# State-space stage of a hybrid block: decays from running sums spread by DMA, y and z kept with features on partitions, one gate and norm per group

## What is computed

```python
u = rmsnorm(h, mix_pre_norm)
q, k, v, z, xbc, dt_raw, g_a, g_b = split(u @ w_in)
y_attn = banded_sink_attention(rope(q), rope(k), v, sinks) @ w_attn_out
# ssd_mixer
x, B, C = split(silu(causal_dwconv(xbc)))
dt = softplus(dt_raw + dt_bias);  a_cs = cumsum(dt * -exp(a_log))
y  = (C B^T * exp(a_cs[l] - a_cs[s]) masked) @ (x * dt)     # diagonal part
y += (C @ previous_state) * exp(a_cs)                       # part from the state
y += x * d_skip
y  = y * silu(z);  y = y * rsqrt(mean(y^2 over the group) + eps) * norm_w
# then
merged = sigmoid(g_a) * y_attn + sigmoid(g_b) * (y @ w_ssd_out)
h = h + rmsnorm(merged @ w_out)
h = h + rmsnorm(silu(conv(gate)) * conv(value) @ w_down)    # channel mixer
```

## Time and profile before

| | |
|---|---|
| median of 3 runs | 1079.98 us (1079.81 to 1080.94) |
| the profiled execution | 1081.87 us, of which the span of instructions is 1079.8 us |
| PE busy | 1059.3 us, 98% of the span |
| DVE, ACT, POOL busy | 645.3, 454.7, 124.6 us |
| groups G = 0 to 3 end (us of the span) | 126.8, 233.0, 339.1, 444.3 |
| granted TensorE clock | 1.00 of 2.4 GHz throughout |

### The profile page before, as it was taken

One profiled execution on the slowest core, in us unless ns is written; L12 is line 12 of the kernel. 1 busy time (PEld: TensorE's weight loads), 2 busy tenths in 40 slices (PEclk: granted clock), 3 DMA queues, 4 the chain that ended last, 5 costly groups with the idle time before them and its releaser, 6 DMA issues.

```text
span 1079.8 us, 13848 instructions
## 1 busy us (share of the span) xinstructions
PE 1059.3 (98%) x5353; PEld 888.5 (82%) x5353; DVE 645.3 (60%) x867; ACT 454.7 (42%) x714; POOL 124.6 (12%) x196
## 2 busy tenths in 40 slices
PE   8999999999999999999999999999999999999997
PEld 8888888878888887788888888788888888888886
DVE  4897777776777777842433233466666666651214
ACT  4664456445654565532321213363434344431112
POOL 6013300330033013200000003120000000000001
PEclk9999999999999999999999999999999999999999
DMA  6321132114202420232233243413424233323211
GB/s 189 118 69 30 40 117 69 30 40 123 81 13 58 138 79 1 79 100 95 78 117 99 96 162 129 137 41 78 116 78 115 80 110 84 110 92 110 82 74 78
DMA packets 108426, 95.39 MB, mean 88 GB/s; under 512 B 12175, under 2 KB 98523, under 8 KB 108379
## 3 DMA queue, kind: packets, MB, share of 16 engines
q1 hardware_dynamic: 108379, 94.74, 28.7%
HBM read 92.63 MB, written 2.10 MB: 88 GB/s over the span
## 4 chain that ended last, share of the span: by engine, by line
PE 85%; DVE 8%; ACT 3%; POOL 2%; issue 1%; DMA 1%; POOLq 0%; DVEq 0%; SPq 0%; ACTq 0%
PE ps L1200 18%; PE ps L1201 18%; PE ps L1202 18%; PE ps L1207 8%; PE ps L1208 8%; PE ps L1209 8%; PE ps L1486 2%; DVE wlo L793 1%; ACT whi L449 1%; DVE conv L902 1%; PE ps L1427 1%; PE ps L1239 1%; POOL xdtd L403 1%; PE ps L1498 1%; PE ps L1478 1%
## 5 line engine op out<-in xcount | busy, mean ns | idle before, releaser
L793 DVE TENSOR_TENSOR wlo<-raw,whi 128x2048 fp32r<-128x2048 f32 (+2 forms) x83 | 188.5, 2272 | 209.8 <-ACT whi L449 209.8
L1200 PE MATMUL ps<-uhi,whi 128*128 128x512 f32 x640 | 249.6, 390 | 0.1
L1202 PE MATMUL ps<-uhi,wlo 128*128 128x512 f32 x640 | 249.1, 389 | 0.0
L1201 PE MATMUL ps<-ulo,whi 128*128 128x512 f32 x640 | 249.0, 389 | 0.0
L449 ACT ACTIVATE whi<-raw 128x2048 fp32r<-128x2048 f32 (+2 forms) x83 | 155.2, 1871 | 175.5 <-PE ps L1209 93.0
L1200 PEld LDWEIGHTS ps<-uhi,whi 128*128 128x128 f32 x640 | 120.2, 188 | 25.1 <-DVE zg L1011 0.2
L1202 PEld LDWEIGHTS ps<-uhi,wlo 128*128 128x128 f32 x640 | 120.1, 188 | 24.9
L1201 PEld LDWEIGHTS ps<-ulo,whi 128*128 128x128 f32 x640 | 120.2, 188 | 24.6
L1207 PE MATMUL ps<-whi,uhi 128*128 128x512 f32 (+2 forms) x304 | 115.3, 379 | 2.0 <-DVE wlo L793 1.8
L1209 PE MATMUL ps<-wlo,uhi 128*128 128x512 f32 (+2 forms) x304 | 112.6, 370 | 0.0
L1208 PE MATMUL ps<-whi,ulo 128*128 128x512 f32 (+2 forms) x304 | 112.6, 370 | 0.0
(11 more groups left out here) (230 smaller groups left out, 1466.9 us busy)
## 6 DMA issues: line engine op xcount, KB each, us to landing
raw<-in_w_in_dram SPq DMA_DIRECT2D x24, 1024.0 KB
raw<-in_w_up_dram SPq DMA_DIRECT2D x44, 512.0 KB
raw<-in_w_down_dram SPq DMA_DIRECT2D x11, 1024.0 KB
raw<-in_w_in_dram SPq DMA_DIRECT2D x16, 512.0 KB
raw<-in_w_ssd_out_dram SPq DMA_DIRECT2D x8, 1024.0 KB
raw<-in_w_attn_out_dram SPq DMA_DIRECT2D x4, 1024.0 KB
raw<-in_w_out_dram SPq DMA_DIRECT2D x4, 1024.0 KB
yT<-in_x_dram SPq DMA_DIRECT2D x4, 512.0 KB, 4.9
```

The source lines that it names most:

```text
L793: dve.tensor_tensor(wlo[sl][:, 0:width] if into is None else into, raw[sl][:, 0:width], h.bitcast(F32), ALU.subtract).then_inc(s["lo_done" ...
L1200: pe.matmul(bank(b)[:, span], hi_[:, k, c], ah[:, span], start=first and k == 0, stop=False)
L1201: pe.matmul(bank(b)[:, span], hi_[:, k, c], al[:, span], start=False, stop=False)
L1202: ins = pe.matmul(bank(b)[:, span], lo_[:, k, c], ah[:, span], start=False, stop=last and k == KD - 1)
```

## The change

- **z** is made by `features` (four tiles of 128 features, all tokens), one in each of four places; two blocks of 8 x 256 in place of 4 x 512. Gate and tanh work on features.
- **Decays.** The running sums of one group, tile and head are written once to a scratch in DRAM (`sum_scr`, and their exponentials beside them), and DMAs copy a row of 8 x 128 of them to all 128 partitions (`sums_bc`, `grow_bc`, 512 KB each). ACT makes `decay_m` from it (`gains`: 8 Relu of 128 x 128 with the token's own sum as bias, then 2 Exp). L1404, L1405, `seg_hi` and `seg_lo` are gone.
- **The part from the state** uses C scaled by POOL per head (`c_dec`, 128 x 1024, 12 times), so that it can be accumulated with the diagonal part. Both are now 8 matmuls with weights 64 wide (`state` or `xdt`) and 128 columns streamed (`products`), and heads take turns between the lower and the upper 64 output partitions.
- **y** comes out with features on partitions, so `turn_y` is gone. One DVE instruction a tile adds the skip term (made by ACT, `skip_x`) and stores y.
- **Gate and norm** are made once per group, in the next group's first blocks: `gate_y` (4 DVE), `square_y` (4 ACT), `sum_squares` (3 DVE), `norm_sums` (4 matmuls of one column), mean, root on POOL, two DMAs through DRAM that spread the roots, `normalize` (4 DVE).
- **Softmax**: Exp reads the scores from PSUM with the maximum as bias and sums on the way (4 ACT with accumulation, and 1 small); the subtraction and the sum over 128 x 512 on DVE are gone.
- **The last tile** of a group has its diagonal part, its `turn_p` and its value product between the four tiles of the next group's first half (of the last group: behind the first matmuls of `gate_a`).

```diff
+            def spread_sums(g, t):
+                sp.wait_ge(s["fell"], 2 * (g * NT + t))
+                sp.dma_start(sums_bc[:, :, :].rearrange("p h l -> p (h l)"), sums_of(g, t)[0].partition_broadcast(P)).then_inc(s["sums_in"], 16)
+
+            def spread_growth(g, t):
+                sp.wait_ge(s["grown"], g * (NT - 1) + t - 1)
+                sp.dma_start(grow_bc[:, :, :].rearrange("p h l -> p (h l)"), sums_of(g, t)[1].partition_broadcast(P)).then_inc(s["grow_in"], 16)
+
+            def spread_roots(g):
+                sp.wait_ge(s["root_ok"], g + 1)
+                sp.dma_start(root_scr[g], small[:, 20:24]).then_inc(s["roots_out"], 16)
+                sp.wait_ge(s["roots_out"], 16 * (g + 1))
+                sp.dma_start(conv[:, 3, :], root_scr[g].rearrange("p t -> (p t)").partition_broadcast(P)).then_inc(s["roots_in"], 16)
...
+                for t in range(2, NT):
+                    spread_sums(g, t)
+                    spread_growth(g, t)
...
+                    pool.wait_ge(s["grow_in"], 16 * (G * (NT - 1) + t + 1))
+                    pool.wait_ge(s["silu_ok"], G * 6 + 2)
+                    pool.wait_ge(s["y_mm"], T + 1 if t else T)
+                    pool.tensor_tensor(c_dec[:, :, :], grow_bc[:, :, :],
+                                       conv[:, 1, (t + 1) * P:(t + 2) * P].unsqueeze(1).to_broadcast([P, SH, P]),
+                                       ALU.mult).then_inc(s["grown"], 1)
...
+                def gains(t, half):
...
+                    if half == 0:
+                        act.wait_ge(s["sums_in"], 16 * (T + 1))
+                        act.wait_ge(s["decay_ok"], 1)
+                        act.wait_ge(s["y_mm"], T)
+                    for h in range(4 * half, 4 * half + 4):
+                        at = G * SH + h
+                        ins = act.activation(decay_m[:, h, :], sums_bc[:, h, :], ACT.Relu, scale=-1.0, bias=sum_s[:, t, at:at + 1])
+                    ins.then_inc(s["fell"], 1)
+                    if half:
+                        for q in range(2):
+                            act.wait_ge(s["fell"], 2 * T + q + 1)
+                            m = decay_m[:, 4 * q:4 * q + 4, :]
+                            act.activation(m, m, ACT.Exp, scale=-1.0).then_inc(s["lexp"], 1)
...
                     act.activation(pT[:, :, :].rearrange("p h l -> p (h l)"), bank(4), ACT.Copy).then_inc(s["pT_sb"], 1)
+                    if t < NT - 1:
+                        gains(t + 1, 0)
                     act.wait_ge(s["o_mm"], T + 1)
                     act.activation(oT[:, bass.ds(G * 2, 2), t * P:(t + 1) * P],
                                    bank(4, 2 * P).rearrange("p (f c) -> p f c", f=2), ACT.Copy, scale=0.5).then_inc(s["o_sb"], 1)
...
+                    if t < NT - 1:
+                        gains(t + 1, 1)
...
+                    dve.tensor_tensor(yT[:, G * 4:G * 4 + 4, c], bank(2 + t % 2).rearrange("p (f c) -> p f c", f=4), conv[:, 2:6, c],
+                                      ALU.add).then_inc(s["y_done"], 1)
...
+            def products(G, t, weights, moving, first, last):
+
+                for h in range(SH):
+                    r = slice((h % 2) * HD, (h % 2 + 1) * HD)
+                    ins = pe.matmul(ps[r, 2 + t % 2, (h // 2) * P:(h // 2 + 1) * P], weights[:, h * HD:(h + 1) * HD],
+                                    moving[:, h, :], start=first if t == 0 else first and h < 2, stop=last if t == 0 else last and h >= SH - 2)
+                return ins
...
+            def norm_sums(G):
+
+                pe.wait_ge(s["sq_ok"], G + 1)
+                pe.wait_ge(s["st_ok"], (G + 1) * (NT - 1))
+                for t in range(NT):
+                    ins = pe.matmul(ps[:, 7, t:t + 1], conv[:, 2, t * P:(t + 1) * P], ones[:, 0:1], start=True, stop=True)
+                ins.then_inc(s["norm_mm"], 1)
...
+                        if h == 0 and t == 0:
+                            diagonal(G - 1, NT - 1)
+                        elif h == 0 and t == 1:
+                            turn_p(G - 1, NT - 1)
+                        elif h == 0 and t == 2:
+                            weigh_values(G - 1, NT - 1)
```

More of the change, by code:

```diff
@@ L121, in hybrid_block @@
[L121 to L125, removed]
+        c_dec = sb("c_dec", [P, SH, P], where=gctx)
+        sums_bc = sb("sums_bc", [P, SH, P], where=gctx)
+        grow_bc = sb("grow_bc", [P, SH, P], where=gctx)
+        probs = sb("probs", [P, QH, P], where=gctx)
+        pT = sb("pT", [P, QH, P], where=gctx)
@@ L941, in group @@
                 lo_next(3)
+                if G:
+                    normalize(G - 1)
                 taps(2)
@@ new lines, in diagonal, with turn_p @@
+            def diagonal(G, t):
+                T = G * NT + t
+                pe.wait_ge(s["m_ok"], T + 1)
+                pe.wait_ge(s["xdt_ok"], T + 1)
+                if t == 0:
+                    pe.wait_ge(s["y_done"], max(T - 1, 0))
+                    pe.wait_ge(s["tok_sb"], G * 5 + 1)
+                products(G, t, xdt, decay_m, t == 0, True).then_inc(s["y_mm"], 1)
+            def turn_p(G, t):
+                pe.wait_ge(s["p_ok"], G * NT + t + 1)
+                for h in range(QH):
+                    ins = pe.transpose(ps[:, 4, h * P:(h + 1) * P], probs[:, h, :], ident[:, :])
+                ins.then_inc(s["pT_mm"], 1)
@@ L1458, in group @@
-                    if t == 0:
-                        z_half(0, 0)
-                        scores()
+                    if t == 0:
+                        z_tile(0)
+                    pe.wait_ge(s["qkT_sb"], G * 3 + 3)
+                    if t:
+                        pe.wait_ge(s["o_sb"], T)
+                        pe.wait_ge(s["sexp"], T * (QH + 1))
+                    else:
+                        pe.wait_ge(s["conv_ok"], G * 6 + 6)
+                    for h in range(QH):
+                        b, o = 4 + h % 2, (h // 2) * P
+                        ins = pe.matmul(ps[:, b, o:o + P], qB[:, h, c], kB[:, c], start=True, stop=True)
@@ L1487, in group @@
-                    ins.then_inc(s["y_mm"], 1)
-                    if t == 0:
-                        sums(1)
-                        turn_p()
+                        pe.wait_ge(s["grown"], G * (NT - 1) + t)
+                        if T > 1:
+                            pe.wait_ge(s["y_done"], T - 1)
+                        if t == 1:
+                            pe.wait_ge(s["tok_sb"], G * 5 + 3)
+                        products(G, t, state, c_dec, True, False)
                     if t < NT - 1:
-                        pe.wait_ge(s["xdtd_ok"], T + 1)
+                        diagonal(G, t)
```

605 lines of the change are left out of this document (297 added, 308 removed).

## The result

The changed kernel takes **1062.57 us** (median of 4 runs, 1061.45 to 1063.64) against 1080.46 us before: ratio 0.983, 95% interval 0.9811 to 0.985, so 17.9 us less. 1057 was forecast, in a range of 1045 to 1074.

What follows compares the result with a forecast made beforehand. PE, busy 98%, bounds the kernel: 61.9 us of its work go, 34.7 come; waits of 10 go, 13.7 come: 23.5 less from 1081.87 is 1058.4. That profiled execution is 1.9 above the median, so 1057, range 1045 to 1074.

Steps and rivals of the forecast that it cites:

- (a): State and diagonal `products`: eight take 0.89 us because the two output halves work at the same time; 28 times, 25.0 us.
- Rival 1: In `products`, the array's halves do not overlap for 128 columns: 25 us come back, 1079 to 1084 us; chance 0.07.
- (b): PE passing between weights 128 and 64 wide: 0.3 us there and back, 20 times, 6.0 us added.
- (c): PE's `norm_sums`, 16 matmuls of one column: 3.5 us added; also a fourth decay matmul, 0.2 us.
- (d): PE's z matmuls: 96 of 512 columns a group before and after, at 0.23 us either way, so 0.
- (e): PE's attention scores wait for ACT's copy giving `o_sb`, now in more tiles: 8 x 0.42, 3.4 us added.
- (f): Tile 3: PE waits 1.0 us for the state and 0.5 for the diagonal part, four times, 6 us added.
- (g): Last group's end, once: DVE's line of 15 to 18 us less PE's 11 us of other matmuls, 4.3 us wait.
- Rival 3: A tile's DVE chain from scores to `turn_p` is the bound: 1 us longer costs 12 us, 1069; chance 0.15.
- the first list: PE work that goes: sums of decays 16.6, `turn_y` 7.3, state part 10.3, diagonal part 27.7, together 61.9 us.

Runs made afterwards that it cites:

- e1_order: Changed kernel with each group of eight products going through the even heads, then the odd, so neighbours write the same output half; 1071.59 us.
- e6_scores: Changed kernel with the two attention scores that need no wait for ACT's copy of the attention output issued first; 1059.16 us.
- e2_seam: Changed kernel with DVE making the rest of the weight block PE waits for ahead of the last group's normalization and splits; 1052.96 us.
- e4_hold: Changed kernel with POOL's `c_dec` in tile 0 of each group held back until DVE has written the probabilities; 1058.27 us.
- b1_half_sums: Kernel before the change, with the matmuls for the low part of the sums of decays left out; 1079.81 us.

## Why the prediction was right, and where it was off

- **(a) halves beside each other**: the mechanism was right. 0.92 to 0.97 us for eight in pairs, 1.02 alone, 0.89 forecast; the 28 come to 27.5 us, 25.0 forecast. Rival 1 is ruled out by the rows and by e1_order.
- **(b) passing between 128 and 64 wide**: 0.3 is about what the rows show. `turn_p` ahead of products takes 0.53 to 0.59 in place of 0.43 to 0.44, the new state 1.06 in place of 0.95 to 1.01. No run has it by itself.
- **(c) `norm_sums`**: 0.81 a group, 3.2 in all, 3.5 forecast. **(d) z** at 0: matmuls of 512 columns start 0.23 apart before and after; no run has z by itself.
- **(e) scores behind `o_sb`**: 0.37 in place of 0.42, 8 times; and a wait that could be taken away (e6_scores).
- **(f) tile 3**: the state cost 3.1 us, 4 forecast, and in the order that was forecast: the rest of `lo`, POOL's `c_dec` (2.50 us), then the state. The row that shows it is the state's scaling, 2.14 us beside `c_dec` in place of 0.69. The 0.5 for the diagonal part did not come.
- **(g) the end of the last group is the term that was mis-sized**: 4.3 forecast, 8.7 measured, and e2_seam takes exactly that back. The line was 18.2 us long (`norm_sums` at 437.2, `wlo` at 455.4), just above my 15 to 18, of which 4.3 took nearly the low end: `norm_sums`, mean and root took 2.6 us where I had 1 for mean and root, the two transfers 6.6, DVE 8.9. That is 1.9 of the 4.4 us, a wait of 6.2. The other 2.5 us, the lower clock behind the wait, were in no term.
- **Rival 3** came true in one tile of four: 2.6 us, and by a single tiny instruction of DVE, not by the length of the chain. It had no term in the sum, and by e4_hold it cost 3.4 us.
- **A steady tile**, from C times B to C times B, is 11.40 us (199.46 to 210.86) against 12.76 (209.90 to 222.66): 1.4 less, 1.6 forecast.

The sum was 23.5 us from trace to trace. The traces differ by 20.1, of which 2.0 is the start: b1_half_sums, whose start is that of the kernel before, reaches the first turn of q and k at 47.22 us, the kernel before in its profiled execution at 49.26. So 18.1 came of the change, 5.4 short. (g) gives 4.4 of it. The other 1.0 is what errors in both directions leave. Too little was taken for (a), by 2.5 us, for tile 0, by 2.6 and more, and for a wait for `pT`, 0.7; and the wait of 0.37 ahead of `turn_y` that I took four times is 0.12 or 0.13 in three groups, 0.7 too much gain. (e) and (f) were 3.3 too dear. The rest, 2 us or more the other way, lies in (b) and in the waits around the work that went, and no run takes it apart. PE's busy time (26.2 us less, 27.2 forecast) doesn't settle it either: it holds the slow matmuls of (g), 2.5 us, and the slow start of the profiled execution before, 1.7. So that everything but (g) came within 1 us is partly luck: the sizes cancel.

Luck is also the ground of the first list, that PE time shed is time gained: b1_half_sums shows that it would have been false for half of the sums of decays taken out alone. The reading that fits is that it held because the change took away the waits of tile 3 along with the work, and those were counted; no run separates the two.

## What to carry to other kernels

Price a wait of TensorE of several us with the lower clock behind it, and look at every once-only seam where a round trip through DRAM stands ahead of work on an in-order engine that feeds TensorE: moving one instruction ahead of it gave 8.7 us here, 2.5 of them the clock's. Where a profile shows an engine at 98%, try how much a small cut of its work brings before adding up a large one. And when GpSimd gets long elementwise work, list which VectorE instructions with both inputs in SBUF can start while it runs: a tiny one on the path can pay as much as a large one (0.16 to 2.41 us here).

## What was not expected of the hardware

- A 128 x 4 addition took 2.41 us beside a GpSimd instruction, and 0.16 without it.
- A wait of PE cost some 0.2 us more than its idle time in the row (0.66 against 0.81 to 0.87, e4_hold).
- The clock fell not only after 6.2 us of standing still, but in b1_half_sums also in the last group, around waits of 0.7, 0.6 and 0.6 us within 3.5 us, to 0.94 and 0.89 over 20 us. In the kernel before 0.1, 0.6 and 0.6 us at the same place left it at 1.00. But the waits alone don't decide: groups 0 to 2 of b1_half_sums have them too (0.7 to 1.0, 0.6, 0.6), and there it stayed at 1.00. What does is open.
- Executions of one kernel start in two ways that are some 2 us apart. In the first microseconds the turns of x come at half the rate in some executions, the profiled one of the kernel before among them (first fence, four records from 7.19 to 8.41), and at full rate in others (second: the changed kernel, eight). b1_half_sums, whose start is the kernel before unchanged, has the fast one too, so the change is not the cause. In the changed kernel with the order of e2_seam the slow start is there as well (first turn of q and k at 49.23). The sums over 7 to 13 us show a granted clock of 1.00 in both; what decides was not tried.

```profile
7.19 1.22 PE L1239 MATMUL ps<-conv,yT 128*128 128x128 f32 x4
```

```profile
7.10 1.16 PE L1331 MATMUL ps<-conv,yT 128*128 128x128 f32 x8
```
